# U phase: both products with the rounded weights as one 512-column matmul, the halves summed on VectorE, and the weighted one-hot rows built on GpSimd

## What is computed

```
def one_chunk(args):
    hc, ic, gc = args
    u_sel = u[ic]
    act = jax.nn.gelu(jnp.einsum('cd,ced->ce', hc, u_sel))
    wts = (gc * act.astype(jnp.float32)).astype(v.dtype)
    return jnp.einsum('ce,ced->cd', wts, v[ic])
```

## Time and profile before

| | us |
|---|---|
| three runs | 2475.28, 2481.26, 2482.69 |
| median | 2481.26 |
| span of the profiled execution | 2477.9 |
| TensorE busy | 2325.2 |
| VectorE busy | 1713.4 |
| ScalarE busy | 1284.3 |
| GpSimd busy | 345.7 |

### The profile page before, as it was taken

The page is one execution under the profiler, slowest core; times in us unless marked ns, Lnnn a source line. Parts: engine busy times, 40 slices in busy tenths (PEclk is TensorE's granted clock), DMA queues, the critical chain, the costliest instruction groups (busy, mean ns, idle before and its releaser), DMA issues.

```text
span 2477.9 us, 50070 instructions
## 1 busy us (share of the span) xinstructions
PE 2325.2 (94%) x17090; PEld 2148.9 (87%) x17090; DVE 1713.4 (69%) x2959; ACT 1284.3 (52%) x2256; POOL 345.7 (14%) x188
## 2 busy tenths in 40 slices
PE   5779999858999889999999999999999999999997
PEld 1338888635698889999999999999999999999997
DVE  7768766787667878888858878877555555555555
ACT  5543224335644347677765565565444444444444
POOL 7440000290001540000021111111000000000000
PEclk7889999969999999999999999999999999999999
DMA  7667886630076555555554444444655555555553
GB/s 266 236 215 255 279 285 231 228 119 1 1 263 229 200 172 182 177 184 178 187 174 158 158 158 157 160 155 158 214 185 179 185 179 185 179 185 179 185 180 116
DMA packets 123895, 453.29 MB, mean 183 GB/s; under 512 B 14400, under 2 KB 15168, under 8 KB 123200
## 3 DMA queue, kind: packets, MB, share of 16 engines
q1 hardware_dynamic: 123840, 452.63, 53.5%
HBM read 448.38 MB, written 4.19 MB: 183 GB/s over the span
## 4 chain that ended last, share of the span: by engine, by line
PE 84%; DVE 6%; issue 6%; POOL 2%; ACT 1%; DMA 0%; DVEq 0%; POOLq 0%; ACTq 0%
PE PS L714 76%; PE PS L987 2%; POOL ada_lo L334 2%; PE PS L868 2%; DVE w_lo L1055 1%; PE PS L842 1%; DVE pr L1300 1%; DVE st L1298 1%; PE PS L856 1%; PE PS L698 1%; PE PS L721 1%; DVE yb L1091 0%; DVE st L1274 0%; ACT w_hi L386 0%; DVE h_l L1085 0%
## 5 line engine op out<-in xcount | busy, mean ns | idle before, releaser
L1055 DVE TENSOR_TENSOR w_lo<-raw,w_hi 128x512 fp32r<-128x512 f32 x1296 | 926.8, 724 | 601.9 <-ACT w_hi L386 586.6
L386 ACT ACTIVATE w_hi<-raw 128x512 fp32r<-128x512 f32 x1296 | 815.7, 630 | 949.9 <-PE PS L714 943.8
L714 PE MATMUL PS<-h_h,w_hi 128*128 128x256 f32 (+1 forms) x2304 | 662.0, 287 | 17.1 <-DVE w_lo L1055 17.1
L714 PE MATMUL PS<-h_h,w_lo 128*128 128x256 f32 (+1 forms) x2304 | 654.2, 284 | 0.0
L714 PE MATMUL PS<-h_l,w_hi 128*128 128x256 f32 (+1 forms) x2304 | 654.2, 284 | 0.0
L714 PE MATMUL PS<-p_hi,w_hi 128*128 128x256 f32 x2048 | 579.7, 283 | 0.0
L714 PE MATMUL PS<-p_lo,w_hi 128*128 128x256 f32 x2048 | 579.6, 283 | 0.0
L714 PE MATMUL PS<-p_hi,w_lo 128*128 128x256 f32 x2048 | 579.6, 283 | 0.0
L714 PEld LDWEIGHTS PS<-h_h,w_hi 128*128 128x128 f32 x2304 | 444.5, 193 | 20.5 <-issue 10.7
L714 PEld LDWEIGHTS PS<-h_l,w_hi 128*128 128x128 f32 x2304 | 444.8, 193 | 0.0
L714 PEld LDWEIGHTS PS<-h_h,w_lo 128*128 128x128 f32 x2304 | 444.2, 193 | 0.0
(11 more groups left out here) (194 smaller groups left out, 2797.1 us busy)
## 6 DMA issues: line engine op xcount, KB each, us to landing
raw<-stream SPq DMA_DIRECT2D x648, 512.0 KB, 3.3
ada<-w_ada SPq DMA_DIRECT2D x192, 512.0 KB, 4.5
x_c<-x_ctx SPq DMA_DIRECT2D x1, 2048.0 KB, 11.3
x<-x_lat SPq DMA_DIRECT2D x1, 2048.0 KB, 10.0
x_scratch<-x SPq DMA_DIRECT2D x1, 2048.0 KB, 7.3
x<-x_scratch SPq DMA_DIRECT2D x1, 2048.0 KB, 9.9
outT<-ot SPq DMA_DIRECT2D x4, 512.0 KB, 2.6
skT<-sk SPq DMA_DIRECT2D x1, 1024.0 KB, 4.8
```

The lines of the kernel that those rows point to most:

```text
L386: nc.scalar.activation(w_hi[:, (2 * j + hf) % SPLIT, :], raw[:, j, hf * HALF:(hf + 1) * HALF], ACT.Copy).then_inc(S["w_high"], 1)
L714: ins = mm(out_, l_, r_, start=(start and q == 0), stop=(stop and q == 2), skip_group_check=check)
L1055: V_.tensor_tensor(w_lo[:, h % SPLIT, :], raw[:, h // 2 % RAW, at_:at_ + HALF], w_hi[:, h % SPLIT, :].bitcast(F32), ALU.subtract).then_inc ...
```

## The change

In each block of the U phase the two matmuls that have w_hi as weights become one: h2_h and h2_l now lie in one tensor `h2_hl`, and one matmul of 512 columns writes w_hi x h2_h to the first half of the bank and w_hi x h2_l to the second. The matmul with w_lo (256 columns) adds to the second half. VectorE sums the halves by a reduction over pairs that lie 256 elements apart, into `A` for tiles below 64 and into `gtmp` from there on, and signals `u_summed`. ScalarE's gelu works in place on that, in SBUF. TensorE waits for `u_summed` before it uses a bank again. The gelus stand later in ScalarE's order (behind the first half unit of the tile after the next). The hotA rows move from VectorE to GpSimd, behind the distance. GpSimd's loop is written out.

```
-        h2_h = at("h2_h", [P, KT, T], F32R, R + 128 * KB)
-        h2_l = at("h2_l", [P, KT, T], F32R, R + 144 * KB)
+        h2_hl = at("h2_hl", [P, 2, KT, T], F32R, R + 128 * KB)
+        h2_h, h2_l = h2_hl[:, 0], h2_hl[:, 1]
...
-            def distance(t0):
+            for g in range(T // 4):
+                if g:
+                    pool.wait_ge(S["route_used"], g)
                 nc.gpsimd.tensor_tensor(hotB[:], iota[:].unsqueeze(1).broadcast_to([P, 4, P]),
-                                        i2T[:, bass.ds(t0, 4)].unsqueeze(2).broadcast_to([P, 4, P]),
+                                        i2T[:, 4 * g:4 * g + 4].unsqueeze(2).broadcast_to([P, 4, P]),
                                         ALU.subtract).then_inc(S["dist_b"], 1)
...
+                for q in range(4):
+                    t = 4 * g + q
+                    ins = nc.gpsimd.tensor_scalar(hotA[:, q, :], iota[:], i1T[:, t:t + 1], gT[:, t:t + 1],
+                                                  ALU.is_equal, ALU.mult)
+                ins.then_inc(S["hot_a"], 1)
...
+            def gelu(i):
+                act.wait_ge(S["u_summed"], i + 3)
+                av = A[:, bass.ds(i, 1), :].rearrange("p a t -> p (a t)")
+                nc.scalar.activation(av, av, ACT.Gelu_apprx_tanh).then_inc(S["gelu_done"], 1)
...
+            def u_tiles(b, first=False):
+                if not first:
+                    gelu(2 * b - 1)
+                split_high(b + 34, 3)
+                split_high(b + 35, 0)
+                gelu(2 * b)
+                split_high(b + 35, 1)
+                split_high(b + 35, 2)
...
+            def routing_tiles(b, first=False, last=False):
+                if first:
+                    gelu(2 * b - 1)
+                else:
+                    gelu_aside(2 * b - 1, 1)
                 split_high(b + 34, 3)
                 one_hot_b(2 * b - (2 * ROUTE_AT - 1))
                 split_high(b + 35, 0)
+                gelu_aside(2 * b, 0)
                 split_high(b + 35, 1)
...
-                            pe.wait_ge(S["gelu_done"], 2 * b + (i + 1))
+                            pe.wait_ge(S["u_summed"], 2 * b + (i + 1))
                         for q in range(4):
                             k = 4 * (h % 4) + q
-                            ins = three(PS[:, i, 0:T], h2_h[:, k, :], h2_l[:, k, :], slice(q * P, (q + 1) * P),
-                                        h % SPLIT, True, k == 0, k == KT - 1)
+                            cols = slice(q * P, (q + 1) * P)
+                            mm(PS[:, i, :], w_hi[:, h % SPLIT, cols], h2_hl[:, :, k, :], start=(k == 0), stop=False,
+                               skip_group_check=True)
+                            ins = mm(PS[:, i, T:2 * T], w_lo[:, h % SPLIT, cols], h2_h[:, k, :], start=False,
+                                     stop=(k == KT - 1), skip_group_check=True)
...
+            def sum_parts(i, bank, dst):
+
+                dve.wait_ge(S["w_free"], 4 * i + (2 * U_U + 4 + SPLIT))
+                V_.reduce_sum(dst, PS[:, bank, :].rearrange("p (a t) -> p t a", a=2), AX).then_inc(S["u_summed"], 1)
...
             def next_low(n):
 
                 for _ in range(n):
+                    at_ = half[0] - 2 * U_U
                     half_low(half[0] // 8, half[0] % 8)
+                    if at_ % 4 == 0 and at_ >= 8:
+                        sum_tile(at_ // 4 - 2, at_ // 4 % 2)
                     half[0] += 1
...
-            dve.wait_ge(S["gelu_done"], 2 * ROUTE_AT + 2)
+            dve.wait_ge(S["gelu_done"], 2 * ROUTE_AT)
...
+            def routing_turn(b, first=False):
                 for s in range(2):
+                    i, g = 2 * b + s, 2 * b + (s - 2 * ROUTE_AT)
+                    blk, h0 = ((b + 34, 4), (b + 35, 0))[s]
+                    half_low(blk, h0)
+                    if not (first and s == 0):
+                        sum_parts(i - 1, 1 - s, gtmp[:, 1 - s, :])
+                    half_low(blk, h0 + 1)
+                    half_low(blk, h0 + 2)
                     route_in(g, s)
+                    half_low(blk, h0 + 3)
+                    if not (first and s == 0):
+                        gelu_in(i - 1, 1 - s, g + 3)
```

More of the change, by code:

```diff
@@ L1490, in _ @@
             next_low(2 * (U_U + 2 + 4 * (GATES_AT + 1)) - half[0])
-            low_turns(34 + GATES_AT + 1, ROUTE_AT - GATES_AT - 1)
+            with dve.Fori(GATES_AT + 1, ROUTE_AT) as b:
+                half_low(b + 34, 4)
+                sum_tile(2 * b - 1, 1)
+                half_low(b + 34, 5)
+                split_low(b + 34, 3)
+                half_low(b + 35, 0)
+                sum_tile(2 * b, 0)
+                half_low(b + 35, 1)
+                split_low(b + 35, 1)
+            sum_tile(2 * ROUTE_AT - 1, 1)
             dve.wait_ge(S["gates_turned"], 1)
@@ L1498, in _ @@
             dve.wait_ge(S["tiles_one"], (NE_TILES - 2 * ROUTE_AT) // 8)
-            dve.wait_ge(S["gelu_done"], 2 * ROUTE_AT + 2)
-            def hot_a(g):
-                for q in range(4):
-                    ins = V_.tensor_scalar(hotA[:, q, :], iota[:], i1T[:, bass.ds(4 * g + q, 1)],
-                                           gT[:, bass.ds(4 * g + q, 1)], ALU.is_equal, ALU.mult)
-                ins.then_inc(S["hot_a"], 1)
+            dve.wait_ge(S["gelu_done"], 2 * ROUTE_AT)
             def route_in(g, s):
                 dve.wait_ge(S["route_used"], g + 1)
-                dve.wait_ge(S["gelu_in"], g + 2)
+                dve.wait_ge(S["gelu_in"], g + 1)
                 av = A[:, :, bass.ds(4 * g, 4)].rearrange("p i t -> p t i")
@@ L1514, in route_in, with gelu_in @@
                                  ).then_inc(S["routed"], 1)
-            def gelu_in(i, s, g):
-                dve.wait_ge(S["gelu_done"], i + 3)
-                dve.wait_ge(S["routed"], g + 3)
+            def gelu_in(i, s, routes):
+                dve.wait_ge(S["gelu_done"], i + 1)
+                dve.wait_ge(S["routed"], routes)
                 av = A[:, bass.ds(i, 1), :].rearrange("p a t -> p (a t)")
@@ L1523, in _ @@
             dve.sem_inc(S["gelu_in"], 2)
[L1525 removed]
+            def routing_turn(b, first=False):
                 for s in range(2):
[L1527 to L1537 removed]
+                    i, g = 2 * b + s, 2 * b + (s - 2 * ROUTE_AT)
[5 more added lines that the diff above has]
+                    half_low(blk, h0 + 2)
+                    route_in(g, s)
+                    half_low(blk, h0 + 3)
+                    if not (first and s == 0):
+                        gelu_in(i - 1, 1 - s, g + 3)
+            routing_turn(ROUTE_AT, first=True)
+            with dve.Fori(ROUTE_AT + 1, 64) as b:
                 routing_turn(b)
[L1539 removed]
+            sum_parts(NE_TILES - 1, 1, gtmp[:, 1, :])
+            gelu_in(NE_TILES - 1, 1, T // 4 + 2)
             def p_low(i, s):
```

64 lines of the change are left out of this document (23 added, 41 removed).

## The result

The changed kernel takes 2494.34 us in the median of five runs (2490.87 to 2500.91), the kernel before 2481.26 us on the same chip. The ratio is 1.0057 with a 95% interval of 1.0041 to 1.0073: slower by 13 us, where 2462 was predicted. The profiled execution has a span of 2494.5 us.

What follows compares the result with a forecast made beforehand. TensorE was taken as the bound, so only less TensorE work would save time. Its gain of 25.8 us, less 4 for the top-16 stretch and 1.3 and 1.4 at the seams, took 2481.3 to 2462 us; own range 2455 to 2468.

Steps and rivals of the forecast that it cites:

- the price of a hotA row on GpSimd: Routed tiles: a row takes 0.45 us, so distance and four rows take 3.0, hidden; range 2.0 to 6.1.
- the rival for it: Routed tiles: hotA rows over 1.08 us make each route wait; at 1.218, 34 us lost, 2496 us; chance 0.07.
- The port: Routed tiles: VectorE's w_lo waits for GpSimd operations reading SBUF; 36 us lost at worst, 2498 us; chance 0.07.
- The gain on TensorE: U phase products: three matmuls of 360.0 ns become two of 347.4; 0.20 us a tile, -25.8 us over 128.
- 2.5 ns per product: U phase products, rival: one matmul less saves only this, not 12.6 ns; gain 5.1 us, 2479 us; chance 0.12.
- The price of the sum on VectorE: One reduction per U tile costs 0.69 us, like one of 512 contiguous elements from the same memory.
- The note on cachelines: Rival on VectorE's sum: distant pairs pay; 1.05 us gives 2483 us, chance 0.17; 1.37 gives 2501, chance 0.04.
- The top-16 stretch: From 918 to about 1240 us, selection, sums and gelu's wait put VectorE just behind TensorE: +4 us.
- The seams: Before the first route +1.3 us, from later copies and hotA; at the end of U +1.4, from gelu's later start.
- my sum: Whole kernel: -25.8 + 4 + 1.3 + 1.4 = -19.1 us, giving 2462 us; chance 0.53.

Runs made afterwards that it cites:

- e9: Changed kernel with VectorE's w_lo subtractions left out in the 64 routed tiles, its waits and signals kept; one execution, 2470.45 us.
- e1: Changed kernel with the hotA rows back on VectorE, between the route's product and the last w_lo of a tile; 2473.95 us, ratio 0.9963.
- e3: Kernel before the change with only the hotA rows moved to GpSimd, products and gelu as before; 2486.31 us, ratio 1.0021.
- e7: e1 with ScalarE's gelu of the first 64 tiles one tile later in its queue; 2471.47 us, ratio 0.9963.
- e8: e6 and e7 together, with the eight zero products at the end of U in another bank order; 2468.12 us, ratio 0.9953.
- e6: e1 with VectorE's wait for the last gelu moved from ahead of the first hotA to right before the first route product; 2469.28 us, ratio 0.9951.
- e11: e8 with the first route's product half a tile later, behind the fourth half of its tile; 2470.04 us, ratio 0.9951.
- e4: Changed kernel with a second hotA buffer, so GpSimd builds rows while a route is pending; 2473.38 us, ratio 0.9965.
- e5: e4 with the two halves of the 512-column operand stored next to each other, as one piece; 2474.65 us, ratio 0.9964.
- e10: e8 with each half's four 512-column products first and then its four 256-column ones; 2470.2 us, ratio 0.9953.

## Why the prediction was wrong, step by step

**The step that failed is the price of a hotA row on GpSimd**, "I take 0.45", and with it "1.22 + 1.8 = 3.0, hidden". I built it from the distance, a quarter of 1.218 with something on top. Measured: 0.79 without w_lo beside it (e9), 1.07 on average in the changed kernel and 1.10 in the middle of the routed tiles, so that distance and rows take 5.53 where I had 3.0. Nor was the 1.218 an undisturbed time: the same distance takes 1.04 in e9 and in e1. The range that I gave reached to 1.218 and held both, and the rival for it gave the time of 2496 us, at a chance of 0.07. I took the value nearest to the more similar operation per element, though nothing in the trace showed such a row. Four of them undisturbed are 3.16 us for 512 elements, three times the 1.04 of the one subtraction over 512. How much of that is a cost of each instruction and how much the other operation, no run separates.

**The second fault lies in the threshold of that rival**, 5.56 us between routes and so 1.08 per row. Distance and rows took 1.14 + 4.39 = 5.53, just within it, and each route waited all the same. I had left out 0.11 of handing over, and 0.28 because a route that TensorE waits for takes 1.17 from start to end, where 0.89 is its pace in a full pipeline. With these, (5.56 - 0.39 - 1.2) / 4 = 0.99 per row is the limit. e3 has 6.65 - 0.89 = 5.76 to give, rows of 0.99, and fits; the changed kernel has rows of 1.10 in the middle, and doesn't.

**The port.** I had it as a rival of its own, with VectorE as the one who waits and 2498 us. The two engines do hold each other up, but in the changed kernel the other one pays: GpSimd, 1.23 us a tile on its rows. Neither the slow rows nor the port alone would have cost anything, by an estimate from these rows: undisturbed rows of 0.79 make 1.04 + 3.16 + 1.17 + 0.11 = 5.48, rows of 0.45 with the 1.23 on top make 1.14 + 1.80 + 1.23 + 1.28 = 5.45, both under the 6.48 of TensorE. The loss took both rivals at once, which neither of my two sums held. The Trainium skill (SBUF — State Buffer, Who interferes with whom) says that a VectorE instruction with two SBUF inputs contends with a GpSimd instruction that reads SBUF, and that the order of issue decides who blocks. The runs agree in the main: rows of 0.79 without w_lo and up to 1.65 with it in the changed kernel, and w_lo of 763 ns beside an undisturbed distance in e1. They don't show it for the other VectorE instruction with two SBUF inputs, gelu_in (A<-A,gtmp): in e9 it overlapped 60 rows by 0.1 to 0.4 us, and none of them took over 0.80, nor did it get longer.

**The gain on TensorE.** Forecast 0.20 us a tile, from 360.0 to 347.4 ns. Measured 346.4 or 353.3, by stretches: 6.48 for a routed tile on average (forecast 6.45, before 6.65), 0.17 gained. At 353.3 it is 0.12, and four fifths of the pairs in the first 64 tiles of the changed kernel ran so. So the size was right at one of the two paces, and what sets the other stays open. The rule of the Trainium skill (TensorE: Matmul & The Clock Gate, Back-to-back issue gap) that I had weighed, 2.5 ns per product, is too small here by more than the pace scatters: 360 less 353.3 is 6.7 ns at the least, 360 less 346.4 is 13.6 at the most.

**The price of the sum on VectorE** was right. It reads pairs 256 elements apart and takes what the reduction of contiguous ones takes, 686 ns:

```profile
L1464 DVE TENSOR_REDUCE gtmp<-PS 128x256 f32<-128x512 f32 x64 | 43.7, 683 | 0.0
```

The note on cachelines in the Trainium skill (SBUF — State Buffer, Door 1) gives PSUM lines of 8 bytes and speaks of matmuls slowed by PSUM accesses that aren't contiguous. I had carried it over to a reduction on VectorE; the measurement decides, and this one isn't slowed.

**The top-16 stretch.** Forecast +4, from gelu's wait for the sum. In the changed kernel the pairs of over 365 ns in the first 64 tiles took 4.9 us beyond 350 each, 37 of them. e7 took gelu's wait away, and of the 5.5 us that it got back some 3.1 were such waits. So the mechanism was right and the size near; what the forecast lacked in this stretch is the slower pace, nearly 6 of the 6.6 us between the 8.8 (64 x 0.20 less 4) of the forecast and the 2.3 gained.

**The seams.** Forecast +1.3 and +1.4, measured +3.0 and +2.7. At the first route the rows alone are more than the missing 1.7, 3.79 and not 1.8:

```profile
1289.89 1.04 POOL L374 TENSOR_TENSOR hotB<-iota,i2T 128x512 f32<-128x512 f32 x1 [31.76 <-DVE gT L1536]
1290.99 3.79 POOL L379 TENSOR_SCALAR hotA<-iota,i1T,gT 128x128 f32<-128x128 f32 x4
```

At the end of U, and behind the first route, TensorE ran slower behind the pause, which I hadn't counted. The eight zero products took 3.35 us and not 1.90 as before, and the first V product started 2.78 us behind the first of them and not 1.85:

```profile
1731.89 3.35 PE L933 MATMUL PS<-zeros 128*128 128x512 bf16 x8 [2.83 <-DVE gtmp L1464]
```

The length of the pause alone doesn't say whether that happens. With 2.34 us of it e8's clock at the first route was 0.66 (as in e6), and e9, with 2.34 us at the end of U, kept 1.00 in each 5 us around it and zero products of 1.90:

```profile
1707.39 1.90 PE L933 MATMUL PS<-zeros 128*128 128x512 bf16 x8 [2.34 <-DVE gtmp L1464]
```

**The sum of it.** With hotA off the chain, the forecast of 2462 was still too low. From the start of U, e1 is 5.7 us shorter than the kernel before, and my sum was 19.1. Of the 13.4 between them the first 64 tiles hold 6.7 (2.1 gained, not 8.8: 64 x 0.08 = 5.1 for the slower pace, the rest gelu), the stretch between the routes 3.5 (9.1 gained, not 12.6: some 1.7 for the clock behind the first route, the rest the pace), the two seams 0.9 and 1.5; 0.8 are left, 0.3 of them behind the first V product. With gelu and the first route mended (e11) the stretch from the start of U is 17.5 us shorter than before, near the 19.1 of my sum, but by mends that the change didn't have.

## What to carry to other kernels

Work that is moved to an idle engine, with one buffer between the two, is safe only if the whole circle fits, from the moment the buffer comes free, through every instruction of the new engine, the two hand-overs, and the consumer's own time from start to end (not its pipelined pace). If it is near the limit, a second buffer can do what a faster operation does: e4 got all of the loss in the routed tiles back with 2 KB per partition, with rows that still took 1.01 on average. An operation that the trace has never shown on an engine should be tried at several prices, one of them by its count of instructions and not its elements, and with the work of its neighbours beside it. And a consumer that reads the producer's newest result in a queue with other work should take the one before it: gelu one tile later cost nothing, took some 3 us of waits away, and the stretch became 5.5 us shorter.

## What the runs showed of the hardware that I had not expected

- A GpSimd tensor_scalar of 128x128 with two per-partition operands takes 789 to 799 ns with VectorE's w_lo left out (e9), where VectorE takes 344 and where GpSimd's own 128x512 subtraction takes 1040.
- Which of GpSimd and VectorE is held up by the other depends on the interleaving. In the changed kernel GpSimd's rows go from 793 to 1069 ns on average beside w_lo, while w_lo keeps 690. In e1 w_lo goes to 763 on average and 1316 at the most, while GpSimd's distance keeps 1042. In the earlier trace rows it was w_lo too, up to 2896 ns.
- A summing reduction of pairs 256 elements apart in the matmul's output memory takes 683 ns for 512, no more than one of contiguous elements (686).
- TensorE's granted clock at a seam: with 1.70 us of idle time it stayed at 1.00, with 2.34 (e8) it was 0.66 in the 5 us in which the route begins, with 2.83 at the end of U 0.72, with 4.74 0.66; but with 2.34 at the end of U (e9) it stayed at 1.00. Where it fell at the first route, the way to the second route took 1.3 (the changed kernel) to 2.4 us (e9) more than between later ones, on top of the idle time. At the end of U the V products began 0.4 (e5) to 1.2 us (e7) later by it, with 2.8 us of idle time in both.
- Pairs of a 512- and a 256-column product run at one of two paces, 346.4 or 353.3 ns, kept from one wait or route to the next. Both are there with either layout (e5); grouping gives one of 350.8 (e10).
